# A change to a two-block transformer kernel on one core: router with stationary weights and folding products, a two-step selection, more weight slots and earlier expert loads

## What is computed

```
grp_prob = jax.nn.softmax((t @ w_grp).astype(F32) + b_grp, axis=-1)
g_prob, g_sel = lax.top_k(grp_prob, 1)
exp_logits = ((t @ w_rtr).astype(F32) + b_rtr).reshape(-1, N_GROUPS, EXP_PER_GROUP)
in_grp = jnp.take_along_axis(exp_logits, g_sel[:, :, None], axis=1)[:, 0]
e_prob, e_sel = lax.top_k(jax.nn.softmax(in_grp, axis=-1), TOP_K_IN_GROUP)
gate = g_prob * e_prob / jnp.sum(e_prob, -1, keepdims=True)
...
hid = jax.nn.silu(jnp.einsum('td,edf->tef', t, w1)) * jnp.einsum('td,edf->tef', t, w3)
y = jnp.einsum('tef,efd->td', hid * combine[..., None].astype(hid.dtype), w2)
```

## Time and profile before

| what | us |
| --- | --- |
| median of three runs | 2215.17 |
| lowest and highest of them | 2214.48, 2221.32 |
| the profiled execution | 2208.44 |
| its span | 2206.6 |
| mean granted clock of TensorE in it | 0.955 |

### The profile page before, as it was taken

The page is one execution under the profiler, slowest core; times in us unless marked ns, Lnnn a source line. Parts: engine busy times, 40 slices in busy tenths (PEclk is TensorE's granted clock), DMA queues, the critical chain, the costliest instruction groups (busy, mean ns, idle before and its releaser), DMA issues.

```text
span 2206.6 us, 36692 instructions
## 1 busy us (share of the span) xinstructions
PE 2012.3 (91%) x14311; PEld 1620.0 (73%) x14315; DVE 937.9 (43%) x1869; ACT 744.4 (34%) x1188; POOL 698.1 (32%) x558
## 2 busy tenths in 40 slices
PE   7989999999999999999999987759999999879866
PEld 6779899998889999987768763324678687734424
DVE  5562436606633456327744341112267553512212
ACT  5554443345645443422323122112223221222212
POOL 6556648885656568810012000000000020000000
PEclk9999999999999999999989988879999999899988
DMA  7335335553444355553300369998423102697793
GB/s 227 103 109 172 115 128 182 179 188 109 134 135 153 115 165 183 169 174 115 115 39 1 129 269 418 421 420 305 162 92 138 39 1 115 259 390 312 293 420 165
DMA packets 196269, 405.95 MB, mean 184 GB/s; under 512 B 18515, under 2 KB 143846, under 8 KB 171286
## 3 DMA queue, kind: packets, MB, share of 16 engines
q1 hardware_dynamic: 192374, 390.20, 48.2%
q0 software_dynamic: 3744, 13.63, 1.6%
HBM read 400.53 MB, written 3.28 MB: 183 GB/s over the span
## 4 chain that ended last, share of the span: by engine, by line
PE 73%; DVE 7%; DMA 7%; ACT 4%; SPq 3%; issue 2%; DVEq 2%; ACTq 1%; POOL 0%; POOLq 0%
PE ps L1009 10%; PE ps L1010 9%; PE ps L1011 9%; PE ps L1340 9%; PE ps L1694 6%; DMA weight_ring<-in_w 5%; SPq L919 3%; PE ps L1605 3%; PE ps L1716 3%; DMA last_pair<-in_w 1%; PE ps L1083 1%; PE ps L1544 1%; DVEq L2231 1%; PE ps L1554 1%; PE ps L1724 1%
## 5 line engine op out<-in xcount | busy, mean ns | idle before, releaser
L2188 POOL TENSOR_TENSOR weight_ring<-weight_ring 128x512 fp32r<-128x512 f32 (+1 forms) x466 | 629.6, 1384 | 316.7 <-ACT weight_ring L1790 297.1
L1009 PE MATMUL ps<-weight_ring 128*128 128x256 f32 x1824 | 531.9, 292 | 19.0 <-DVE acts L2305 8.4
L1011 PE MATMUL ps<-weight_ring 128*128 128x256 f32 x1568 | 442.3, 282 | 0.0
L1010 PE MATMUL ps<-acts,weight_ring 128*128 128x256 f32 x1472 | 418.3, 284 | 0.0
L1009 PEld LDWEIGHTS ps<-weight_ring 128*128 128x128 f32 x1824 | 347.9, 191 | 32.7 <-issue 27.8
L1011 PEld LDWEIGHTS ps<-weight_ring 128*128 128x128 f32 x1568 | 301.3, 192 | 0.0
L1010 PEld LDWEIGHTS ps<-acts,weight_ring 128*128 128x128 f32 x1472 | 281.6, 191 | 1.9 <-issue 1.4
L1790 ACT ACTIVATE weight_ring<-weight_ring 128x2048 fp32r<-128x2048 f32 x128 | 238.7, 1883 | 84.9 <-PE ps L1011 75.7
L1340 PE MATMUL ps<-acts,weight_ring 128*128 128x272 f32 x896 | 212.8, 396 | 2.7 <-ACTq L2138 1.4
L2210 POOL CAST row_of<-slot_token 128x1 uint32 (+1 forms) x26 | 5.0, 190 | 635.5 <-PE ps L1672 426.4
L1340 PEld LDWEIGHTS ps<-acts,weight_ring 128*128 128x128 f32 x896 | 170.5, 191 | 40.8 <-issue 2.4
(11 more groups left out here) (465 smaller groups left out, 3723.2 us busy)
## 6 DMA issues: line engine op xcount, KB each, us to landing
weight_ring<-in_w SPq DMA_DIRECT2D x120, 1024.0 KB, 23.4
weight_ring<-in_w_gate_up SPq DMA_DIRECT2D x44, 1024.0 KB, 5.1
acts<-in_w SPq DMA_DIRECT2D x40, 1024.0 KB, 25.4
...
```

Of the source, the lines that this page charges most:

```text
L1009: nc.tensor.matmul(o, wh, xh, start=start, stop=False)
L1010: nc.tensor.matmul(o, wh, xr, start=False, stop=False)
L1011: return nc.tensor.matmul(o, wr, xh, start=False, stop=stop)
L2188: nc.gpsimd.tensor_tensor(r12(w), w, r12(high[:, n % HIGH, part]).bitcast(F32), ALU.subtract).then_inc(rest_ready, 1)
```

## The change

It has these parts.

- **Slots and loads.** XS becomes 22: a new buffer `spare` holds two more loads; `std` and `rstd` now lie at its end. Ten loads of group 1 go before the loop. Six are issued during the mixer, w_out, norm and router products ((1,8), (1,6), (1,7), (1,5), (1,2), (1,1)); then the token rows are written out, and (1,3), (1,9), (1,4) and (1,0) follow.
- **Router.** The 32 columns of `router_w` in a window from column 0 or 4 are stationary, the 272 tokens move. Chunks 4a to 4a+3 go to four column groups side by side, so a bank then holds four partial sums in its partitions. ACT copies bank `ra` and DVE bank `rb` to SBUF; six products with `fold_logits` (four unit matrices of 32 below each other, added) sum the four parts and turn them back to tokens in rows. One token tile's transposes stand in between.
- **Starts.** The eight additions one after another become a product with a triangular table, a sum and one addition, and `slots_out(start)` comes ahead of the last.
- **Selection two steps ahead.** Before the loop two selections, with ten filling products, in the loop that of s + 2, between the two halves of the down product. The bank counts change from three to two uses.
- **First block.** ACT casts the third bay and makes the root before the rope's sine; DVE's memory norm moves from head group 3 to 2; two memory chunks instead of one before `S[1]`; one cast of the memory attention moves one place; the B output projection makes its first two column groups together, and waits for the scaled quarters one by one.
- **Bacc** is told `dynamic_dma_scratch_size=2048`.

The diff, cut (of the load loop the old lines are in the listing above; the slot map, semaphore and bank bookkeeping and the building of `fold_logits` from the identity, three additions at the block's start, are left out):

```diff
@@ -138,7 +138,7 @@
-        XS = 20
+        XS = 22
@@ -151,8 +151,8 @@
-        std = sb("std", [P, S2])
-        rstd = sb("rstd", [P, S2])
+        spare = sb("spare", [P, 4096])
+        std, rstd = spare[:, 4096 - 2 * S2:4096 - S2], spare[:, 4096 - S2:4096]
@@ -584,10 +590,10 @@
-                order += [S[0], *memory[:1], S[1], *memory[1:], N[0], N[1]]
+                order += [S[0], *memory[:2], S[1], *memory[2:], N[0], N[1]]
...
-                    if g == 3:
+                    if g == 2:
@@ -600,7 +606,7 @@
-            return [("split", "xq", 0), ("split", "xq", 1), ("S", 0), ("T", 0), ("split", "xq", 2), ("S", 1), ("T", 1), ("split", "xq", 3),
+            return [("split", "xq", 0), ("split", "xq", 1), ("S", 0), ("T", 0), ("split", "xq", 2), ("S", 1), ("split", "xq", 3), ("T", 1),
@@ -729,7 +735,7 @@
-            return s * 3 + (3 * l + 3 + nth)
+            return s * 3 + (2 * l + 2 + nth)
@@ -918,40 +928,38 @@
+                    for tile, places in ((("sv", l, 2), ((0, 0), (0, 1), (1, 8))),
+                                         (("od", l, 2), ((0, 4), (0, 5), (0, 6), (0, 7), (1, 6))),
+                                         (("aO", l, 2), ((0, 2), (0, 3))),
+                                         (("wo", l, 7), ((0, 8), (0, 9), (0, 10), (0, 11), (1, 7))),
+                                         (("mu", l, 0), ((1, 5),)), (("va", l, 0), ((1, 2),)), (("rt", l), ((1, 1),))):
+                        b, u = tiles[tile]
+                        sp.wait_ge(full[b], u)
+                        for g, m in places:
+                            expert_load(g, m)
+                    b, u = tiles[("ht", l, 2, 1)]
+                    sp.wait_ge(full[b], u)
+                    sp.wait_ge(htok_ready, 6 * (l + 1))
+                    for n, (t0, L) in enumerate(TOK):
+                        sp.dma_start(h_rows[t0:t0 + L, :], h_tok[0:L, n, :]).then_inc(rows_out, 16)
+                    sp.wait_ge(comb_ready, l + 1)
+                    expert_load(1, 3)
+                    expert_load(1, 9)
+                    sp.wait_ge(rows_out, 48 * (l + 1))
+                    expert_load(1, 4)
+                    b, u = tiles[("rk", l)]
+                    sp.wait_ge(full[b], u)
+                    expert_load(1, 0)
+                    for g in range(1, 8):
+                        for m in range(10 if g == 1 else 0, 12):
...
+                            if m0 == 0:
...
+                            elif m0 == 8:
@@ -1264,12 +1272,20 @@
-                if kind == "B":
-                    pe.wait_ge(sub_done, 4)
-                else:
+                if kind == "A":
...
-                    project(("o", l, g), o_src)
+                    if kind == "A" or g > 1:
+                        project(("o", l, g), o_src)
+                    elif g == 0:
+                        scaled = set()
...
+                        def o_scaled(k):
+                            if k % 2 == 0 and k not in scaled:
+                                scaled.add(k)
+                                pe.wait_ge(sub_done, k // 2 + 1)
+                            return o_src(k)
+                        project_together([("o", l, 0), ("o", l, 1)], o_scaled)
@@ -1616,24 +1632,39 @@
-                hold_clock(begin("rt", l), 12)
+                hold_clock(begin("ra", l), 12)
...
-                b = begin("rt", l)
+                part_banks = [begin("ra", l), begin("rb", l)]
...
-                    for n in (0, 2, 1):
-                        t0, L = TOK[n]
-                        for k in range(4 * a, 4 * a + 4):
...
-                            last = nc.tensor.matmul(ps[0:L, b, 36 * n:36 * n + 36], hT[:, k, t0:t0 + L], router_w[:, k, :],
-                                                    start=(n == 0 and k == 0), stop=(n == 1 and k == KT - 1))
+                    for b, c0 in zip(part_banks, (0, 4)):
+                        for j in range(4):
+                            k = 4 * a + j
+                            last = nc.tensor.matmul(ps[32 * j:32 * j + 32, b, 0:S2], router_w[:, k, c0:c0 + 32], hT[:, k, :],
+                                                    start=(a == 0), stop=(a == 1))
+                        if a:
+                            last.then_inc(full[b], 1)
...
+                def turn_tokens(n, c):
...
+                    t0, L = TOK[n]
+                    b = begin("ht", l, n, c)
+                    for k in range(4):
+                        last = nc.tensor.transpose(ps[0:L, b, k * P:(k + 1) * P], hT[:, 4 * c + k, t0:t0 + L], ident)
+                    last.then_inc(full[b], 1)
...
+                turn_tokens(0, 0)
+                pe.wait_ge(logit_parts_ready, 2 * (l + 1))
+                b = begin("rt", l)
+                for n in (0, 2, 1):
+                    t0, L = TOK[n]
+                    nc.tensor.matmul(ps[0:L, b, 36 * n:36 * n + 32], std[:, t0:t0 + L], fold_logits[:, :], start=True, stop=True)
+                    last = nc.tensor.matmul(ps[0:L, b, 36 * n + 32:36 * n + 36], rstd[:, t0:t0 + L], fold_logits[:, 28:32], start=True, stop=True)
...
-                for n, (t0, L) in enumerate(TOK):
+                for n in range(3):
...
-                        b = begin("ht", l, n, c)
-                        for k in range(4):
-                            last = nc.tensor.transpose(ps[0:L, b, k * P:(k + 1) * P], hT[:, 4 * c + k, t0:t0 + L], ident)
-                        last.then_inc(full[b], 1)
+                        if (n, c) != (0, 0):
+                            turn_tokens(n, c)
@@ -1672,15 +1703,14 @@
-                for n in range(3):
-                    if n:
-                        hold_clock(begin_l(ROWS[0], row_use(start, l, -1)), 14 if n == 1 else 3)
-                    pe.wait_ge(sel_ready, start + (3 * l + 1 + n))
-                    slots(start + n, up_use(start, l, n - 3))
-                hold_clock(begin_l(ROWS[0], row_use(start, l, -1)), 3)
+                pe.wait_ge(sel_ready, start + (2 * l + 1))
+                slots(start, up_use(start, l, -2))
+                hold_clock(begin_l(ROWS[0], row_use(start, l, -1)), 10)
...
+                pe.wait_ge(sel_ready, start + (2 * l + 2))
+                slots(start + 1, up_use(start, l, -1))
@@ -1716,6 +1746,9 @@
+                        if a == 0:
+                            pe.wait_ge(sel_ready, s + (2 * l + 3))
+                            slots(s + 2, up_use(s, l, 2))
@@ -1730,8 +1763,6 @@
-                    pe.wait_ge(sel_ready, s + (3 * l + 4))
-                    slots(s + 3, up_use(s, l, 2))
@@ -1900,11 +1931,13 @@
+                    first_highs(3)
+                    norm_root(n0)
...
-                    first_highs(3)
+                    first_highs(HIGH)
@@ -1913,9 +1946,8 @@
-                        norm_root(n0)
-                        if l == 0:
-                            first_highs(HIGH)
+                        if l:
+                            norm_root(n0)
@@ -2137,6 +2169,9 @@
+                b = filled("ra", l)
+                nc.scalar.activation(std[:, :], ps[:, b, 0:S2], ACT.Copy).then_inc(logit_parts_ready, 1)
+                nc.scalar.drain().then_inc(free[b], 1)
@@ -2206,7 +2241,7 @@
-                    pool.wait_ge(slots_ready, s + (3 * l + 1))
+                    pool.wait_ge(slots_ready, s + (2 * l + 1))
@@ -2784,6 +2823,11 @@
+                nc.vector.tensor_tensor(up_to, edges[:, 0:8].unsqueeze(2).broadcast_to([P, 8, 8]),
+                                        edges[:, 0:8].unsqueeze(1).broadcast_to([P, 8, 8]), ALU.is_ge)
+                b = filled("rb", l)
+                nc.vector.tensor_copy(rstd[:, :], ps[:, b, 0:S2]).then_inc(logit_parts_ready, 1)
+                nc.vector.drain().then_inc(free[b], 1)
@@ -2877,12 +2921,14 @@
-                for g in range(8):
-                    nc.vector.scalar_tensor_tensor(out=starts[:, g + 1:g + 2], in0=passes[:, g:g + 1], scalar=1.0, in1=starts[:, g:g + 1],
-                                                   op0=ALU.add, op1=ALU.add)
-                    settle()
...
-                slots_out(start, up_use(start, l, -2))
+                nc.vector.tensor_tensor(over_edge[:, :, :], up_to, passes[:, :].unsqueeze(1).broadcast_to([P, 8, 8]), ALU.mult)
+                settle()
+                nc.vector.reduce_sum(passes[:, :], over_edge[:, :, :], AX.X)
+                slots_out(start, up_use(start, l, -1))
+                settle()
+                nc.vector.scalar_tensor_tensor(out=starts[:, 1:9], in0=passes[:, :], scalar=starts[:, 0:1], in1=count[:, 1:9],
+                                               op0=ALU.add, op1=ALU.add)
+                settle()
@@ -2910,14 +2956,13 @@
-                for n in (1, 2):
-                    select_at(start + n)
-                    slots_out(start + n, up_use(start, l, n - 2))
+                select_at(start + 1)
+                slots_out(start + 1, up_use(start, l, 0))
...
-                    select_at(s + 3)
+                    select_at(s + 2)
```

(5 more changed lines are left out.)

52 lines of the change are left out of this document (19 added, 33 removed).

## The result

The changed kernel takes 2180.0 us in the median of four runs (2174.7 to 2181.7), the kernel before 2215.4 (2214.5 to 2221.3). The ratio is 0.983, 95% interval 0.981 to 0.986: 35 us less. A second measurement gave 2179.7 against 2212.5 (0.985, 0.984 to 0.987). The profiled execution took 2179.8; the forecast on that basis was 2179.1, on the median's 2186.

A forecast was written before the change was run, and what follows sets the result against it. PE, with 73% of the chain, bounds the kernel; edits pay only where it idles or runs at half clock. First block −8.9, first layer −6.95, second −13.4 give −29.3: 2179.1 us on the profile, 2186 on the median, range 2168 to 2205.

The forecast's parts named there:

- Two more slots, loads in front: Expert loop: DMA-bound windows each end 5.0 us sooner, −5.0 in the first layer and −10.0 in the second.
- Router: Router products: 16 wide calls plus copies and folding take about 4.5 us in place of 6.7, −2.2.
- the rival of groups one after another: Router products: the four column groups do not overlap, +5.5 us a layer, 2197 us; chance 0.04.
- starts: Between router and gather: eight additions become a multiply, a sum and one addition, slots read out earlier, −1.1 us.
- Gather and first up product: After the router: gather issued 3.3 us sooner, median landing 8.9; up product earlier by 3.75 (first layer) and 5.2 (second).
- Clock: First up product of each layer: with ten filling calls PE idles and it starts cold, +1.8 us a layer.
- Start: First block: the bay's cast and root go ahead of the rope's sine, first rotary product 2.6 us earlier.
- Memory norm: First block: norm one head group earlier removes PE's wait near 141 us, less a sixth charged to the softmax, −2.3 us.
- Output projections: First block: made two at a time, each waiting only for the quarter it reads, −4.0 us.
- In the step: Expert loop: slot product moves between the down product's halves, gather leaves later but lands in time, 0 with 0.9 to spare.
- Quick gather: Rival: first gather lands in about 4.0 us and PE stays at full clock, 2172.5 us; chance 0.14.
- Late gather in every step: Rival, slower side: PE's transposes wait for gathers in 13 of 24 steps, up to +40, 2226 us; chance 0.08.

The follow-up runs named there:

- run 1: The changed kernel again with no edit, to show what varies between executions: 2179.7 us.
- run 2: The changed kernel with XS back to 20 slots instead of 22, so 8 early loads of group 1 instead of ten: 2189.1 us.
- run 3: The changed kernel with all ten loads of group 1 issued late, once the gates are there, 22 slots kept: 2189.2 us.
- Run 7: The changed kernel with the old router products (24 calls, tokens stationary, no folding): 2191.7 us.
- run 8: The changed kernel with 18 filling calls instead of 10 ahead of the first transposes: 2181.3 us.
- run 9: The changed kernel with the whole first block's orders and waits put back as in the kernel before: 2188.4 us.
- run 5: The changed kernel with slot product and read-out back between the halves of the scatter products, selection still two steps ahead: 2187.8 us.
- run 10: The changed kernel with the last four early loads held until the first gather landed, and all nine step-loop bounds read ahead of the first group: 2185.3 us.
- run 4: The changed kernel with the last four loads ahead of the loop held until the first gather has landed: 2173.9 us.

## Why the prediction was right

The sign and the place in the range hold, and most terms of the sum do: −29.3 forecast, −28.7 between the two profiled executions, −33 to −35 between medians. The profiled execution of the kernel before was at the low end of its runs, so the 6.7 us that I added for the median did not carry over.

That −29.3 and −28.7 are so close is in part luck. The two traces differ by −5.0 up to the first layer's router (1279.85 to 1274.86; forecast −8.9), by −5.2 from there to the first layer's last up product (−6.95), by −5.1 from there to the second layer's router (339.1 to 334.0; forecast 0, since the change leaves this stretch as it was but for the rest of one step and the early loads), and by −13.7 in the second layer's router and loop (−13.4). The first block did bring its share: the traces are 8.0 apart at 680 us, but 3.0 of it are lost again by 1240, in stretches where two traces of one kernel differ as well (run 1). The third part is mostly the drop near 1760 (run 1) that the trace of the kernel before has and this one has not. The sum had no term for either, and the two nearly make up for each other. By the steps of the prediction:

*Two more slots, loads in front:* forecast −5.0 and −10.0; measured −5.1 to −5.4, −6.0 and −4.8, and run 2 gives them back. The best-founded term, a size from the rate of a window, was the exact one. It is the worth of the windows, though, not of the slots in the whole: run 2 costs 9 and not 16, since fewer loads stand before the first gathers then. The early issue of the loads, for which I gave no sum of its own, is worth something by itself (run 3).

*Router:* forecast −2.2; measured −2.8 (6.75 to 3.97), 2.04 for the products against 1.9. The row of another product with four groups side by side was the right price; the rival of groups one after another has fallen. The *starts* and the rest bring the gather's issue forward by 3.5 and 4.3, forecast 3.3. Run 7 gives 2.6 and 3.1 of it to the router, which leaves 0.9 and 1.3 for the starts (forecast −1.1); no run undoes those alone.

*Gather and first up product:* forecast −3.75 and −5.2; measured −2.9 and −6.1. The median landing (8.9) was the right one to take. *Clock:* forecast +1.8; the up product was 1.3 and 1.4 longer in the first trace, 2.7 and 0 in the second. That transposes and slot product run cold too (in the first layer, 1.97 for 1.04) I had left out. With PE kept busy (run 8) all of them are warm, the up product 7.07 in both layers. The rule of the Trainium skill (TensorE: Matmul & The Clock Gate, "HAM oscillation — how this bites in real kernels"), that products after a wait which left the array idle start cold, agrees with that. What it costs in the total stays open (run 8).

*Start:* forecast −2.6, measured −1.9 (run 9; 2.0 between the two first traces, from 45.24 to 43.25). I let DVE's reciprocal begin as soon as ACT had the root. It stands behind the rope's arguments on DVE, and these got slower. DVE, POOL and PE rows after:

```profile
26.01 1.22 DVE L2439 TENSOR_SCALAR rope<-rot_tmp 128x256 f32<-128x256 f32 x1
27.15 1.37 DVE L2440 TENSOR_SCALAR rot_tmp<-rot_tmp 128x256 f32<-128x256 f32 x1
28.60 0.29 DVE L2442 TENSOR_SCALAR rot_tmp<-rot_tmp 128x256 f32<-128x256 f32 x1
...
30.37 1.74 DVE L2309 RECIPROCAL rstd_u<-spare 128x256 f32<-128x256 f32 x1
...
17.52 10.85 POOL L2223 TENSOR_TENSOR weight_ring<-weight_ring 128x512 fp32r<-128x512 f32 x8 [0.51 <-ACT weight_ring L1916]
...
43.25 2.08 PE L1130 MATMUL ps<-qkv 64*128 64x256 f32 x8 [3.91 <-DVE qkv L2478]
```

and DVE and POOL before:

```profile
24.44 0.29 DVE L2404 TENSOR_SCALAR rope<-rot_tmp 128x256 f32<-128x256 f32 x1
...
17.85 5.24 POOL L2188 TENSOR_TENSOR weight_ring<-weight_ring 128x512 fp32r<-128x512 f32 x4 [0.63 <-ACT weight_ring L1885]
```

The same operation on 128 x 256 takes 0.29 while POOL is idle and 1.2 to 1.4 while POOL subtracts (until 28.4). The earlier cast gave POOL work in just this stretch. The Trainium skill (SBUF — State Buffer, "SBUF: two separate sides") says that GpSimd and a DVE operation that either runs in a two-port mode or has two inputs in SBUF share one pair of ports, which one of them holds for a whole instruction. The trace agrees, by 0.29 against 1.22, if these operations are of that kind, which it does not show; and the reciprocal takes 1.75 beside POOL (before, where POOL works from 30.25) and 1.74 without it.

*Memory norm:* forecast −2.3, measured about −0.3. This term of the sum failed, though the total did not show it. I charged a sixth of the norm to the softmax of the group before, because its probabilities had seemed ready in time. PE rows after:

```profile
127.81 0.66 PE L1139 MATMUL ps<-tables,probs 128*128 128x128 f32 x4 [1.40 <-DVE probs L2382]
...
137.31 1.14 PE L1130 MATMUL ps<-qkv 64*128 64x256 f32 x8 [1.07 <-DVE qkv L2478]
140.43 0.35 PE L1017 MATMUL ps<-weight_ring 128*128 128x256 f32 x1 [1.98 <-DVE acts L2340]
```

The wait at 141 fell from 5.09 to 1.98, worth 3.8 with the clock. But against run 9 PE had lost 3.5 between 60 and 137 us, in waits for DVE (1.40 and 1.07 here): nearly the whole norm, 4.0, not a sixth. DVE was the chain there.

*Output projections:* forecast −4.0, measured −5.0. Two small order changes, for which the sum had no term, brought 0.6 and 1.6 (run 9, at 262 and 635). So the first block is 9.6 by run 9, forecast 8.9: errors of both signs that cancel, which is luck too.

*In the step:* forecast 0, measured +0.25 a step and +0.85 at a change of group: 1.8 in the first layer's end, 1.6 in the second's. The part that I reckoned with 0.9 to spare held. What the view of the gather's line shows after:

```profile
who waited for it (us, times):
  PEld ps L1703: 11.2, 5
  PE ps L1703: 7.8, 2
...
DMA to landing us min/median/max: 4.2/8.6/9.8
```

Two waits of PE, both at the first gathers, and none in the loop; run 5 shows how close it is. What I missed is what the slot product had covered where it stood, the reading of the bounds at a change of group: 0.6, which run 10 takes away (16.97 again). The 0.25 lies in the products themselves. The down product in two halves and the slot product between them take 4.62 in the chain above (1.92, 0.85, 1.85). Before, the down product was one piece and the slot product stood later; the chain of that kernel:

```profile
1544.46 3.64 PE ps L1716 x32
...
1549.61 0.73 PE ps L1665 x6
```

That is 4.37. Run 5, with the slot product back in its old place, has 3.64 and 0.73 to 0.75 again. The Trainium skill (TensorEngine Tiling (Array Packing), "Key Properties") says that a change of tiling mode drains the engine. The old place was among other full products (128*128); the new one makes PE go from column groups (128*32) to full products and back within the down product. That fits, but no run separates it from other causes.

*Quick gather*, the rival of 2172.5, did not come by itself, but it is real: run 4 makes it, at 2173.9. *Late gather in every step*, the rival on the other side, is what run 5 makes of it, +8 in place of +40: of the 13 steps that I counted only five wait, 8.1 us together, since the others find few loads queued or stand where the DMA bounds the time anyway.
